# Loading the second expert matrix of the first token tile ahead of the routing table, in a one-core trunk step

## The chip, the cores and the metric

The kernel runs on one core of one Trainium2 chip. The metric is the device time of one execution in microseconds; where a median is given, it is that of three executions. TensorE is called PE, VectorE DVE, ScalarE ACT, GpSimd POOL and SyncE SP. PE multiplies; DVE and ACT do elementwise work; SP issues most of the weight loads; POOL issues the gathers of token rows.

## The reference

One layer of a decoder trunk for 512 prompt tokens and 8 sample tokens, all in float32. A token mixer comes first, then the sub-layer that this change concerns, a mixture of 16 experts in 4 groups, with two experts for each token:

```
gidx = argmax(softmax(hf @ rg + rg_b))            # one group of four
sel  = logits of the four experts of that group
tv, ti = top_k(softmax(sel), 2)                   # two experts inside the group
for e in range(16):
    act = silu(hf @ w1[e]) * (hf @ w3[e])         # w1, w3: 1024 x 512
    y  += (act @ w2[e]) * comb[:, e]              # w2: 512 x 1024
x = x + g2 * y                                    # then a final RMSNorm
```

## The kernel before

**Tiles.** The kernel sorts the 1040 (token, expert) choices into tiles of 128 rows, each for a single expert. In this run there are 18 tiles. Which expert a tile belongs to is known only once the routing table (`table`, `tile_expert`, `fresh_flags`) has been worked out by DVE; the first tile always belongs to expert 0, since no expert is left out of the sort.

**Weights and their ring.** A matrix of an expert (2 MB) comes in four quarters of 512 KB (128 partitions x 1024 floats). A turn of the ring has `TURN = 12` quarters: six places in `raw` and six in `more_raw` (five in `region_a`, one in `region_b`). Before PE can use a quarter, ACT copies it rounded into `w_hi` (`hi`, L1096) and DVE takes the rest into `w_lo` (`lo`, L1519); both have `SPLIT = 4` places. PE then does three products for each pair (`three`, L636 to L638), since operands of the reduced kind are split in two parts.

**Order of the expert stage.** Turn 0 holds w1 and w3 of tile 0 and w1 of tile 1 (ring numbers 0 to 3, 4 to 7, 8 to 11, SP L596, L599, L610). Turn j, from 1 on, holds w3 of tile j, w2 of tile j-1 and w1 of tile j+1 (SP L614 to L617). So the second matrix of tile 0, w2[0], is used in turn 1, at ring numbers 4 to 7. A load whose matrix is the same expert's as the tile's before is left out and only its mark is set by a 4-byte transfer (`kept_mark`, L581). The loops over turns run with register counters, on SP, PE, ACT and DVE alike.

**What stands ahead of the loop.** While the second norm and the routing run, SP loads w1 and w3 of tile 0 and eight quarters of another matrix, the last two column groups of w_ada (`gap_load`, L587), whose products (`gap_products`, L932) fill gaps on PE. The last three of them are issued after `h2_ready` (L600 to L603). Then SP waits for the table (L604), for the first gather and for the gap products (L608, L609), and loads w1 of tile 1.

**Rows of a tile.** The normed token rows h2 are stored to DRAM (L1290, from three buffers in `region_b` that take turns; the traces call the DRAM tensor h_rows). For each tile POOL gathers 128 rows of 4 KB from it into `xg` in `region_b` (L1460, an indirect DMA), PE turns them (L1021 for the first tile, L980 after), ACT and DVE split them into `hT_hi` and `hT_lo`. The first gather needs only the list of expert 0's tokens and starts before the table is complete. The second needs the full list, which DVE and PE work out after the first gather has been turned: split of the first rows (L1978 to L1980), `tile_parts` (L1984), the product in `list_tokens` (L988), `slot_tokens` (L1989), `slot_idx` (L1892). POOL sets `second_begun` (L1467) after it has issued the second gather, and SP starts the loads of turn 1 only then (L613).

SP's, ACT's and POOL's transfers run on the same 16 DMA engines, in three queues: q1 (SP), q10 (ACT), q0 (POOL).

Of the kernel before, what the change touches and what calls it, by code (L numbers as in the profile page):

```python
# [22 lines left out]
P = 128  # L23
# [6 lines left out]
NTILE = NP // P + 1  # L30
# [11 lines left out]
KF = FF // P  # L42
# [8 lines left out]
QUARTER = 1024  # L51
TURN = 12
# [19 lines left out]
N_EXP = N_WO + 8  # L72
# [16 lines left out]
def trunk_step(nc, x_prompt, x_sample, state_conf, state_pool, state_sconv, c_prompt, c_sample, w_ada,  # L89
# [9 lines left out]
    with ctx:  # L99
        def sb(name, shape, dt=F32):  # L100
            return ctx.enter_context(nc.sbuf_tensor(name, shape, dt))

        def sem(name):
            return ctx.enter_context(nc.semaphore(name))
# [3 lines left out]
        w_hi = sb("w_hi", [P, SPLIT, QUARTER], F32R)  # L108
        w_lo = sb("w_lo", [P, SPLIT, QUARTER], F32R)
# [4 lines left out]
        region_b = sb("region_b", [P, 13500])  # L114
# [24 lines left out]
        table = sb("table", [P, 3], I32)  # L139
        kept_mark = sb("kept_mark", [1, TURN], I32)  # L140
        tile_expert = sb("tile_expert", [P, MAX_TILES], I32)

        fresh_flags = sb("fresh_flags", [P, 2, MAX_TILES], I32)
# [6 lines left out]
        def carve(region, at, *dims):  # L150
            n = int(np.prod(dims))
            v = region[:, at:at + n]
            if len(dims) == 2:
                return v.rearrange("p (a b) -> p a b", b=dims[1])
            if len(dims) == 3:
                return v.rearrange("p (a b c) -> p a b c", b=dims[1], c=dims[2])
            return v
# [5 lines left out]
        def raw_place(n, turn=None):  # L163

            if n < N_APART:
                count, step = 1, TURN // RAW
                place, ready = nat_place[n], apart_ready[n]  # L170
            elif n < N_EXP:
                m = n - N_APART
                count, step = m // RAW + 1, TURN // RAW
                place = raw[:, m % RAW, :]
                ready = raw_ready[m % RAW]
            else:
                c, base = n - N_EXP, N_EXP - N_APART
                if c % TURN < RAW:
                    s = (base + c % TURN) % RAW
                    place, ready = raw[:, s, :], raw_ready[s]  # L180
                    count = (base - s + RAW - 1) // RAW + c // TURN + 1
                else:
                    place, ready = more_raw[c % TURN - RAW], more_ready[c % TURN - RAW]
                    count = c // TURN + 1
                step = 1
            return place, ready, 16 * count if turn is None else turn * (16 * step) + 16 * count

        def split_slot(n):

            return (n - (n > N_MIX)) % SPLIT  # L190

        def splits(n):

            return n + 1 - (n > N_MIX)
# [51 lines left out]
        g2_dec = carve(region_b, 11264, D)  # L246
        yg = [carve(region_b, at, 2, D) for at in (9216, 0, 5120, 7168)]
        more_raw.append(carve(region_b, 2048, QUARTER))
        gap_place = [carve(region_b, 7168, QUARTER), carve(region_b, 8192, QUARTER), carve(region_b, 11264, QUARTER), more_raw[4],
                     carve(region_b, 6144, QUARTER), more_raw[2], more_raw[3], more_raw[5]]  # L250
        g2_rows = g2_dec[0:ND + 1, :]
# [41 lines left out]
        lo_done = sem("lo_done")  # L293
# [45 lines left out]
        h2_stored = [sem(f"h2_stored{i}") for i in range(3)]  # L339
        h2T_done = sem("h2T_done")  # L340
# [17 lines left out]
        table_ready = sem("table_ready")  # L358
        xg_ready = sem("xg_ready")
        second_begun = sem("second_begun")  # L360
        gather_free = sem("gather_free")
        xgT_done = sem("xgT_done")
        silu_ready = sem("silu_ready")
# [97 lines left out]
        def _(sp):  # L461
# [64 lines left out]
            for b, w in enumerate((sc_out, conf_pw)):  # L526
                for q in range(4):
                    n = N_MIX + 1 + 4 * b + q
# [4 lines left out]
            for h in range(2):  # L533
                for q in range(4):
                    n = N_WO + 4 * h + q
# [51 lines left out]
            def gap_load(h):  # L587

                g, q = G_ADA - 1 - h // 4, 2 * (h % 4)
                sp.dma_start(gap_place[h].rearrange("p (k n) -> p k n", k=2), ada_v[:, q:q + 2, g * COLS:(g + 1) * COLS]).then_inc(nat_ready[h], 16)  # L590
# [10 lines left out]
            gap_load(5)  # L601
            gap_load(6)
            gap_load(7)  # L603
            sp.wait_ge(table_ready, 6)  # L604
            last = sp.value_load(table[0:1, 1:2], min_val=NE - 1, max_val=MAX_TILES - 1)
            before_last = sp.value_load(table[0:1, 2:3], min_val=NE - 2, max_val=MAX_TILES - 2)
# [4 lines left out]
            sp.dma_start(g2_bias, b_ada[0, 5 * D:6 * D].partition_broadcast(ND + 1)).then_inc(ld_mod, 16)  # L611

            sp.wait_ge(second_begun, 1)  # L613
            with sp.Fori(1, last) as j:  # L614
                where_fresh(up_weights, 0, exp_w3, bass.ds(j, 1), j, 1)
                where_fresh(down_weights, 4, None, bass.ds(j - 1, 1), j, 0)
                where_fresh(up_weights, 8, exp_w1, bass.ds(j + 1, 1), j, 0)  # L617
# [462 lines left out]
        def _(act):  # L1080
# [5 lines left out]
                ins.then_inc(act_step, 1)  # L1086
                act.wait_ge(act_step, steps[0])

            def hi(n, turn=None):


                place, ready, count = raw_place(n, turn)
                act.wait_ge(ready, count)
                if splits(n) > SPLIT or turn is not None:
                    act.wait_ge(quarter_used, splits(n) - SPLIT if turn is None else turn * TURN + (splits(n) - SPLIT))
                act.activation(w_hi[:, split_slot(n), :], place, ACT.Copy).then_inc(hi_done, 1)  # L1096
# [175 lines left out]
            def his(first, end, j=None):  # L1272
                for c in range(first, end):
                    hi(N_EXP + c, j)
# [50 lines left out]
            def silu_tile(j):  # L1325

                act.wait_ge(quarter_used, TURN * j + splits(N_EXP - 1))
                act.wait_ge(act_ready, j)
                act.activation(silu_t, ps[:, 0, :], ACT.Silu).then_inc(silu_ready, 1)

            def turned_rows_out(j):
                act.wait_ge(xgT_done, j + 1)
                act.activation(xgT_hi, ps[:, 2:4, :].rearrange("p b (k t) -> p (b k) t", k=4), ACT.Copy).then_inc(xgT_hi_done, 1)
# [18 lines left out]
            last = act.value_load(table[0:1, 1:2], min_val=NE - 1, max_val=MAX_TILES - 1)  # L1352
# [13 lines left out]
            his(10, 12)  # L1366
            turned_product_out(0)
            his(12, 15)
            with act.Fori(1, last) as j:
                his(3, 4, j)  # L1370
                silu_tile(j)
                his(4, 8, j)
                turned_rows_out(j + 1)
                his(8, 11, j)
                y_out(j - 1, TURN * j + splits(N_EXP + 7))
                turned_product_out(j)
                his(11, 12, j)
                y_store(j, j - 1)
                his(12, 15, j)
            his(3, 4, last)  # L1380
            silu_tile(last)
            his(4, 11, last)
# [22 lines left out]
            for i in range(NTILE + 2):  # L1405
                if i < NTILE:
                    scale_first(i)
                if i >= 2:
                    t = i - 2
                    n = rows(t)  # L1410
# [75 lines left out]
        def _(dve):  # L1486
# [30 lines left out]
            def rest(out, whole, first):  # L1517

                return dve.tensor_tensor(out, whole, first.bitcast(F32), ALU.subtract)  # L1519

            def lo(n, turn=None):

                count = splits(n) if turn is None else turn * TURN + splits(n)

                dve.wait_ge(hi_done, count)
                rest(w_lo[:, split_slot(n), :], raw_place(n)[0], w_hi[:, split_slot(n), :]).then_inc(lo_done, 1)


            dve.memset(cT[:, :, 16:C_LO].bitcast(F32), 0.0)
# [84 lines left out]
            for n in range(5):  # L1614
                lo(n)
# [110 lines left out]
            for n in range(N_HEAD + 6, N_MIX):  # L1726
                kind, g = ITEMS[n // 4]
                q = 4 * g + n % 4 if kind == "z" else -1
# [95 lines left out]
            def los(first, end, j=None):  # L1824
                for c in range(first, end):
                    lo(N_EXP + c, j)
# [42 lines left out]
            for i in range(NTILE + 1):  # L1869
# [6 lines left out]
                    row_means(i, i, NTILE + i + 1, 3 + i)  # L1876
                if i >= 3:
                    logit_tile(i - 3)
            dve.memset(fresh_flags[:, 0, 0:1], 1)
            dve.memset(fresh_flags[:, 1, 0:2], 1)  # L1880
            dve.tensor_copy(tile_f, tile_no[:, 0:MAX_TILES])
            dve.tensor_scalar(tile_start[:, :], tile_no[:, :], float(P), None, ALU.mult)
# [59 lines left out]
            count, tiles = ps[:, 7, NTILE * NE:(NTILE + 1) * NE], tiles16[:, 8:]  # L1942
# [10 lines left out]
            link(dve.tensor_tensor(ended, ends[:, None, :].broadcast_to([P, MAX_TILES, NE]), tile_f[:, :, None].broadcast_to([P, MAX_TILES, NE]), ALU.is_le))  # L1953
            link(dve.tensor_reduce(tile_f, ended, AX.X, ALU.add))
            dve.tensor_copy(tile_expert[:, :], tile_f).then_inc(table_ready, 1)
            for flags, first in ((0, 1), (1, 2)):
                dve.tensor_tensor(fresh_flags[:, flags, first:], tile_f[:, first:], tile_f[:, first - 1:MAX_TILES - 1], ALU.not_equal).then_inc(table_ready, 1)
            dve.tensor_scalar(table[:, 1:2], ends[:, NE - 1:NE], -1.0, None, ALU.add).then_inc(table_ready, 1)
            dve.tensor_scalar(table[:, 2:3], ends[:, NE - 1:NE], -2.0, None, ALU.add).then_inc(table_ready, 1)
# [35 lines left out]
            def product_tile(j, used):  # L1995

                dve.wait_ge(quarter_used, used)
                dve.wait_ge(silu_ready, j + 1)
                dve.wait_ge(actT_done, j)
                dve.tensor_tensor(act_t, ps[:, 1, :], silu_t, ALU.mult).then_inc(act_ready, 1)  # L2000
# [10 lines left out]
            last = dve.value_load(table[0:1, 1:2], min_val=NE - 1, max_val=MAX_TILES - 1)  # L2011
# [14 lines left out]
            link(dve.reciprocal(share[:, 0, :], col1[:, :, 4]))  # L2026
            link(dve.tensor_tensor(share[:, 1, :], share[:, 0, :], col1[:, :, 5], ALU.mult), share_ready, 1)
            los(12, 15)
            with dve.Fori(1, last) as j:
                los(3, 7, j)  # L2030
                product_tile(j, TURN * j + splits(N_EXP + 3))
                los(7, 8, j)
                turned_rows_rest(j + 1)

                list_out(bass.ds(j + 2, 1))
                los(8, 11, j)
                turned_product_rest(j)
                los(11, 15, j)
            los(3, 7, last)
            product_tile(last, TURN * last + splits(N_EXP + 3))  # L2040
            los(7, 11, last)
# [12 lines left out]
            for i in range(NTILE + 2):  # L2054
                if i < NTILE:
                    n = rows(i)
# [42 lines left out]
```

## Time and profile before

| | |
|---|---|
| median of 3 executions | 883.67 us (883.58 to 884.1) |
| the profiled execution: its time | 885.43 us |
| the profiled execution: its span | 883.6 us |
| PE busy | 820.7 us, 93% of the span |
| DVE busy | 681.3 us, 77% |
| ACT busy | 467.0 us, 53% |
| DMA moved | 201.21 MB, mean 228 GB/s |
| mean granted clock of PE | 0.968 |

Starts are counted from the span's start. The expert stage begins near 507 us, with the first gathered rows. PE's share of the chain that ended last is 81%. The DMA share is high in the first slices of the span and from about 500 us to 830 us. A release named in brackets is what ended an idle time.

### The profile page before, as it was taken

The page shows a single profiled execution, that of the slowest core. Times are in us where ns is not written, and L with a number is a line of the kernel's source. Part 1 is how long each engine was busy: PE and PEld are TensorE (multiplying, and loading weights), DVE is VectorE, ACT ScalarE, POOL GpSimd, SP SyncE. Part 2 cuts the span into 40 slices and gives each one's busy share as a digit, 9 for nine tenths or more (in the row PEclk, how much of TensorE's full clock was granted, in tenths as well). Part 3 has the DMA queues.
Part 4 walks back from the last instruction along what each step waited for, and adds up shares of the span by engine and source line. Part 5 has one row for each costly group of instructions (what it writes and reads, how often), then busy time and mean ns, then how long its engine had stood idle before and what let it go on. Part 6 is the DMA issues. An engine that isn't in the chain of part 4 may idle for free.

```text
span 883.6 us, 14769 instructions
## 1 busy us (share of the span) xinstructions
PE 820.7 (93%) x4987; PEld 692.2 (78%) x4987; DVE 681.3 (77%) x933; ACT 467.0 (53%) x551; POOL 50.1 (6%) x58
## 2 busy tenths in 40 slices
PE   7899999999999999999999989999999999999810
PEld 2589999989899999899776367888888888888700
DVE  0782637978797786698358879998999989998748
ACT  4552442343422221642223368888888888888642
POOL 0002000000000000230000010001000100000040
PEclk9889999999999999999999999999999999999955
DMA  9858535445543321223752489978978899999462
GB/s 331 278 166 284 196 119 165 127 159 167 170 127 115 96 73 48 69 82 120 270 188 96 169 324 397 397 269 299 387 305 317 320 399 400 396 397 401 171 217 96
DMA packets 90963, 201.21 MB, mean 228 GB/s; under 512 B 8760, under 2 KB 13368, under 8 KB 90886
## 3 DMA queue, kind: packets, MB, share of 16 engines
q1 hardware_dynamic: 78813, 165.25, 53.0%
q0 software_dynamic: 4960, 17.89, 5.6%
q10 hardware_dynamic: 7147, 17.47, 5.3%
q8 instruction: 29, 0.48, 0.2%
q14 instruction: 14, 0.11, 0.0%
HBM read 182.44 MB, written 18.87 MB: 228 GB/s over the span
## 4 chain that ended last, share of the span: by engine, by line
PE 81%; DVE 8%; DMA 4%; ACT 2%; issue 2%; ACTq 1%; SPq 1%; POOL 0%; POOLq 0%; DVEq 0%
PE ps L785 31%; PE ps L636 13%; PE ps L638 13%; PE ps L637 13%; PE ps L865 3%; PE ps L980 2%; DMA region_a<-in_x_prompt_dram 2%; DMA region_b<-h_rows,slot_idx 2%; PE ps L817 2%; DVE w_lo L1519 1%; PE ps L664 1%; PE ps L665 1%; ACT w_hi L1096 1%; PE ps L1015 1%; DVE region_b L2061 1%
## 5 line engine op out<-in xcount | busy, mean ns | idle before, releaser
L1519 DVE TENSOR_TENSOR w_lo<-raw,w_hi 128x1024 fp32r<-128x1024 f32 x202 | 241.4, 1224 | 100.3 <-ACT w_hi L1096 98.3
L1096 ACT ACTIVATE w_hi<-raw 128x1024 fp32r<-128x1024 f32 x202 | 207.9, 1056 | 197.4 <-PE ps L785 150.6
L636 PE MATMUL ps<-w_hi,hT_hi 128*128 128x512 f32 (+1 forms) x512 | 205.2, 401 | 5.4 <-DVE hT_lo L1519 3.7
L638 PE MATMUL ps<-w_hi,hT_lo 128*128 128x512 f32 (+1 forms) x512 | 202.1, 395 | 0.0
L637 PE MATMUL ps<-w_lo,hT_hi 128*128 128x512 f32 (+1 forms) x512 | 201.6, 394 | 0.0
L785 PE MATMUL ps<-hT_hi,w_hi 128*128 128x260 f32 x768 | 156.4, 285 | 1.7 <-DVE w_lo L1519 0.9
L785 PE MATMUL ps<-hT_hi,w_lo 128*128 128x260 f32 x768 | 155.0, 283 | 0.0
L785 PE MATMUL ps<-hT_lo,w_hi 128*128 128x260 f32 x768 | 155.0, 283 | 0.0
L785 PEld LDWEIGHTS ps<-hT_hi,w_hi 128*128 128x128 f32 x768 | 118.9, 189 | 5.0 <-DVE w_lo L1519 3.9
L785 PEld LDWEIGHTS ps<-hT_lo,w_hi 128*128 128x128 f32 x768 | 119.4, 190 | 0.0
L785 PEld LDWEIGHTS ps<-hT_hi,w_lo 128*128 128x128 f32 x768 | 118.9, 189 | 0.0
L636 PEld LDWEIGHTS ps<-w_hi,hT_hi 128*128 128x128 f32 (+1 forms) x512 | 94.6, 185 | 29.8 <-issue 4.0
L638 PEld LDWEIGHTS ps<-w_hi,hT_lo 128*128 128x128 f32 (+1 forms) x512 | 94.5, 184 | 24.1
L1519 DVE TENSOR_TENSOR w_lo<-region_a,w_hi 128x1024 fp32r<-128x1024 f32 x90 | 108.4, 1219 | 5.2 <-ACT w_hi L1096 4.6
L637 PEld LDWEIGHTS ps<-w_lo,hT_hi 128*128 128x128 f32 (+1 forms) x512 | 94.7, 185 | 22.5
L1096 ACT ACTIVATE w_hi<-region_a 128x1024 fp32r<-128x1024 f32 x90 | 95.5, 1062 | 28.3 <-PE ps L638 28.3
L1666 DVE SCALAR_TENSOR_TENSOR region_b<-region_b,pT 128x512 f32<-128x512 f32 x120 | 81.7, 735 | 0.0
L1519 DVE TENSOR_TENSOR hT_lo<-ps,hT_hi 128x512 fp32r<-128x512 f32 (+1 forms) x37 | 34.4, 933 | 16.2 <-ACT hT_hi L1349 12.9
L1460 POOL DMA_INDIRECT region_b<-h_rows,slot_idx x18 | 20.8, 1154 | 383.2 <-DVE slot_idx L1892 273.6
L1203 ACT ACTIVATE region_a<-ps 128x520 f32<-128x520 f32 x24 | 14.5, 606 | 33.7 <-PE ps L785 33.7
L1439 POOL TENSOR_TENSOR hT_lo<-region_b,hT_hi 128x520 fp32r<-128x520 f32 x8 | 12.0, 1525 | 299.4 <-ACT hT_hi L1211 275.5
L664 PE MATMUL ps<-w_hi,cT 128*48 128x512 f32 x64 | 27.0, 422 | 2.0 <-DVE w_lo L1519 1.7
(307 smaller groups left out, 788.0 us busy)
## 6 DMA issues: line engine op xcount, KB each, us to landing
raw<-in_exp_w_dram SPq DMA_DIRECT2D x96, 512.0 KB
region_a<-in_exp_w_dram SPq DMA_DIRECT2D x80, 512.0 KB
raw<-in_w_in_dram SPq DMA_DIRECT2D x48, 512.0 KB
raw<-in_w_ada_dram SPq DMA_DIRECT2D x30, 512.0 KB
expert_rows<-region_b ACTq DMA_DIRECT2D x18, 512.0 KB, 6.5
region_b<-in_exp_w_dram SPq DMA_DIRECT2D x16, 512.0 KB
region_b<-in_w_ada_dram SPq DMA_DIRECT2D x14, 512.0 KB, 9.2
expert_rows<-region_a POOLq DMA_DIRECT2D x8, 512.0 KB, 8.1
```

Of the source, the lines that this page charges most:

```text
L636: pe.matmul(out, pairs[0], moving[0], start=start, stop=False)
L637: pe.matmul(out, pairs[0], moving[1], start=False, stop=False)
L638: return pe.matmul(out, pairs[1], moving[0], start=False, stop=stop)
L664: pe.matmul(ps[0:C_LO + 16, bank, :], cT[:, kk, :], hi[:, k, :], start=(kk == 0), stop=False)
L785: mm = pe.matmul(ps[:, 2 * m + h, 0:HT], w[:, k, ms], x[:, kk, h * HT:(h + 1) * HT], start=start, stop=stop)
L817: mm = pe.matmul(ps[:, 2 * s + h, 0:HT], lhs(k), rhs(k)[:, h * HT:(h + 1) * HT], start=(k == 0), stop=(k == n - 1))
L865: mm = pe.matmul(ps[:, 2 * s + h, 0:HT], w[:, k, (t % 2) * P:(t % 2 + 1) * P], x[:, kk, h * HT:(h + 1) * HT], start=start, stop=stop)
L980: t = pe.transpose(ps[:, 2 + k // 4, (k % 4) * P:(k % 4 + 1) * P], xg[:, k * P:(k + 1) * P], ident[:, :])
L1096: act.activation(w_hi[:, split_slot(n), :], place, ACT.Copy).then_inc(hi_done, 1)
L1460: pool.indirect_dma_start(xg, None, h2_dram, bass.IndirectOffsetOnAxis(ap=slot_idx[:, :], axis=0)).then_inc(xg_ready, 16)
L1519: return dve.tensor_tensor(out, whole, first.bitcast(F32), ALU.subtract)
L1666: dve.scalar_tensor_tensor(va[:, c, 0:NP], ua[:, c, t:t + NP], w, va[:, c, 0:NP], ALU.mult, ALU.add).then_inc(conv_step, 1)
```

## The change

Four places of 512 KB in `region_b` get a second use, `early_raw`: two that held vectors for the sample tokens (9216, 10240) and two of the three h2 buffers (0, 1024). SP loads w2 of expert 0 into them right after the last gap loads and ahead of its wait for the table. It waits first until the five h2 tiles have been turned by PE and the two buffers' stores to DRAM have landed. Turn 1 is written out of the loops on SP, ACT and DVE; the loops begin at 2. In turn 1 ACT and DVE split the quarters 4 to 7 from the early places. The ring's places keep their count of marks, so SP sets four marks there. The flag of turn 1 for w2 is no longer computed. PE's and POOL's code is not touched.

```
+        early_raw = [carve(region_b, at, QUARTER) for at in (9216, 10240, 0, 1024)]
...
             gap_load(5)
             gap_load(6)
             gap_load(7)
+            sp.wait_ge(h2T_done, NTILE)
+            sp.wait_ge(h2_stored[0], 32)
+            sp.wait_ge(h2_stored[1], 32)
+            for q in range(KF):
+                sp.dma_start(early_raw[q], exp_w2[0, 0, q * P:(q + 1) * P, :]).then_inc(early_ready, 16)
             sp.wait_ge(table_ready, 6)
...
             sp.wait_ge(second_begun, 1)
-            with sp.Fori(1, last) as j:
+            where_fresh(up_weights, 0, exp_w3, slice(1, 2), 1, 1)
+            for q in range(4, 8):
+                _, ready, _ = raw_place(N_EXP + q)
+                sp.dma_start(kept_mark[0:1, q:q + 1], table[0:1, 0:1]).then_inc(ready, 16)
+            where_fresh(up_weights, 8, exp_w1, slice(2, 3), 1, 0)
+            with sp.Fori(2, last) as j:
...
-            def hi(n, turn=None):
+            def hi(n, turn=None, early=None):
-                place, ready, count = raw_place(n, turn)
+                place, ready, count = raw_place(n, turn) if early is None else (early_raw[early], early_ready, 64)
...
-            with act.Fori(1, last) as j:
+            def turn_of(j, early=False):
                 his(3, 4, j)
                 silu_tile(j)
-                his(4, 8, j)
+                if early:
+                    for q in range(KF):
+                        hi(N_EXP + 4 + q, j, q)
+                else:
+                    his(4, 8, j)
...
+            turn_of(1, early=True)
+            with act.Fori(2, last) as j:
+                turn_of(j)
...
-            def lo(n, turn=None):
+            def lo(n, turn=None, early=None):
-                rest(w_lo[:, split_slot(n), :], raw_place(n)[0], w_hi[:, split_slot(n), :]).then_inc(lo_done, 1)
+                place = raw_place(n)[0] if early is None else early_raw[early]
+                rest(w_lo[:, split_slot(n), :], place, w_hi[:, split_slot(n), :]).then_inc(lo_done, 1)
...
-            with dve.Fori(1, last) as j:
-                los(3, 7, j)
-                product_tile(j, TURN * j + splits(N_EXP + 3))
-                los(7, 8, j)
+            def turn_of(j, early=False):
+                los(3, 4, j)
+                for q in range(KF):
+                    lo(N_EXP + 4 + q, j, q if early else None)
+                    if q == 2:
+                        product_tile(j, TURN * j + splits(N_EXP + 3))
```

On SP, from the fourth gap load on to the loads of w1 of tile 1, before (region_b and raw are SBUF, in_w_ada_dram and in_exp_w_dram the weights in DRAM):

```order
L590 DMA region_b<-in_w_ada_dram 128x2x512
L472 DMA region_a<-in_exp_w_dram 128x2x512 x2
L590 DMA region_a<-in_w_ada_dram 128x2x512 x2
L590 DMA region_b<-in_w_ada_dram 128x2x512
L605 TENSOR_LOAD table
L605 ISA x2
```

and after:

```order
L593 DMA region_b<-in_w_ada_dram 128x2x512
L475 DMA region_a<-in_exp_w_dram 128x2x512 x2
L593 DMA region_a<-in_w_ada_dram 128x2x512 x2
L593 DMA region_b<-in_w_ada_dram 128x2x512
L611 DMA region_b<-in_exp_w_dram 128x1024 x4
L613 TENSOR_LOAD table
L613 ISA x2
```

Four loads of a quarter each stand between the last gap load and the reading of the table.

On ACT, from the end of turn 0 into turn 1, before (w_hi is the rounded copy, and L1369 is the loop's head):

```order
L1349 ACTIVATE hT_hi<-ps 128x4x128
L1096 ACTIVATE w_hi<-raw 128x1024 x3
L1369 UNCONDITIONAL_BRANCH
L1369 ISA
L1095 ISA
L1096 ACTIVATE w_hi<-raw 128x1024
L1329 ACTIVATE region_b<-ps 128x512
L1095 REGISTER_ALU
L1096 ACTIVATE w_hi<-raw 128x1024
```

and after:

```order
L1362 ACTIVATE hT_hi<-ps 128x4x128
L1109 ACTIVATE w_hi<-raw 128x1024 x4
L1342 ACTIVATE region_b<-ps 128x512
L1109 ACTIVATE w_hi<-region_b 128x1024 x4
L1346 ACTIVATE hT_hi<-ps 128x8x128
L1109 ACTIVATE w_hi<-region_a 128x1024 x3
```

The four copies of w2[0] stand where they stood and read another place; the loop's head has moved one turn further on.

## Rows read from the trace of the kernel before

**Rows 1.** Windows: busy us by engine, clock, DMA share, GB/s, by stage.
```profile
495.50:501.40 5.90, 5.30 (x34) 1.53 (x32) 4.44 (x24) 0.80 (x3) 0.00 (x0) 1.00 0.94 308
501.40:506.80 5.40, 4.46 (x10) 0.89 (x10) 4.99 (x19) 0.00 (x0) 1.02 (x1) 1.00 0.48 170
...
513.00:521.20 8.20, 6.93 (x30) 5.26 (x28) 6.30 (x7) 6.96 (x7) 1.18 (x1) 1.00 1.01 340
...
527.00:584.00 57.00, 56.20 (x264) 45.66 (x263) 52.74 (x57) 47.38 (x51) 3.48 (x3) 1.00 1.04 398
584.00:830.00 246.00, 246.00 (x1145) 201.06 (x1144) 226.41 (x219) 207.09 (x218) 13.93 (x12) 1.00 0.92 347
```
**Rows 2.** Waits of PE, 495 to 880 us: us in total, times, longest.
```profile
PE ps L636 <- DVE hT_lo L1519: 3.7, 2, 2.7
PE ps L980 <- DMA region_b<-h_rows,slot_idx: 1.3, 1, 1.3
PE ps L932 <- DMA region_a<-in_w_ada_dram: 0.8, 1, 0.8
PE ps L636 <- DVE w_lo L1519: 0.8, 1, 0.8
PE ps L1021 <- DMA region_b<-h_rows,slot_idx: 0.6, 1, 0.6
```
**Rows 3.** Chain of waits, 497 to 533 us: start, us, what.
```profile
501.41 5.41 DMA region_b<-h_rows,slot_idx
...
506.86 0.67 PE ps L1021 x4
...
508.18 1.29 DVE hT_lo L1519 x2
...
513.03 8.15 DMA region_b<-h_rows,slot_idx
```
**Rows 4.** Timeline of SP's queue: start, us of issuing, operation.
```profile
495.05 0.47 SPq L590 DMA_DIRECT2D region_b<-in_w_ada_dram  x1
509.70 1.53 SPq L472 DMA_DIRECT2D region_a<-in_exp_w_dram  x3
...
514.80 5.98 SPq L472 DMA_DIRECT2D raw<-in_exp_w_dram  x6
```
**Rows 5.** DMA issues of the page: stores of h2 rows.
```profile
h_rows<-region_b ACTq DMA_DIRECT2D x4, 512.0 KB, 2.6
```
**Rows 6.** The line of the gathers, all 18: issue to landing.
```profile
DMA to landing us min/median/max: 5.4/7.5/8.2
```
**Rows 7.** DMA issues at 525 to 526, then at 614 to 615 us: us to landing.
```profile
region_b<-h_rows,slot_idx POOLq DMA_INDIRECT x1, 7.7
```
```profile
region_b<-h_rows,slot_idx POOLq DMA_INDIRECT x1, 6.2
```
**Rows 8.** Groups from 500 us on, by form: splits by place.
```profile
L1519 DVE TENSOR_TENSOR w_lo<-raw,w_hi 128x1024 fp32r<-128x1024 f32 x106 | 124.9, 1220 | 4.6 <-ACT w_hi L1096 2.8
...
L1519 DVE TENSOR_TENSOR w_lo<-region_b,w_hi 128x1024 fp32r<-128x1024 f32 x18 | 22.1, 1225 | 4.3 <-ACT w_hi L1096 4.3
```
**Rows 9.** Windows of PE alone: busy us, granted clock, DMA share, GB/s.
```profile
488.00:492.00 4.00, 3.75 (x27) 0.99 0.08 14
492.00:495.40 3.40, 3.23 (x20) 0.51 0.30 108
831.00:835.00 4.00, 1.27 (x9) 1.00 0.32 131
840.00:843.50 3.50, 2.40 (x7) 1.00 0.32 130
```
**Rows 10.** Timeline of PE: gap products.
```profile
487.31 1.89 PE L932 MATMUL ps<-region_b,small 128*16 128x512 f32 x4
...
492.71 3.18 PE L932 MATMUL ps<-region_b,small 128*16 128x512 f32 x4
...
505.25 1.02 PE L932 MATMUL ps<-region_b,small 128*16 128x512 f32 x2
```

More of the change, by code:

```diff
@@ L360, in trunk_step @@
         second_begun = sem("second_begun")
+        early_ready = sem("early_ready")
         gather_free = sem("gather_free")
@@ L1878, in _ @@
                     logit_tile(i - 3)
-            dve.memset(fresh_flags[:, 0, 0:1], 1)
+            dve.memset(fresh_flags[:, 0, 0:2], 1)
             dve.memset(fresh_flags[:, 1, 0:2], 1)
@@ L1955, in _ @@
             dve.tensor_copy(tile_expert[:, :], tile_f).then_inc(table_ready, 1)
-            for flags, first in ((0, 1), (1, 2)):
+            for flags, first in ((0, 2), (1, 2)):
                 dve.tensor_tensor(fresh_flags[:, flags, first:], tile_f[:, first:], tile_f[:, first - 1:MAX_TILES - 1], ALU.not_equal).then_inc(table_ready, 1)
@@ L2038, in _ @@
                 los(11, 15, j)
+            turn_of(1, early=True)
+            with dve.Fori(2, last) as j:
+                turn_of(j)
             los(3, 7, last)
```

## The prediction

> **What bounds the kernel now.** I read the windows by stage first. From 527 us to 584 us PE is busy for 56.20 of 57.00 us and from 584 us to 830 us for all of it, although the DMA engines are just as full there (share 1.04 and 0.92) [rows 1]. Then I read PE's waits from 495 us on. They are 7.4 us in all: 3.7 and 0.8 us for DVE, 1.3 and 0.6 us for gathered rows, 0.8 us for a gap load, and what is left is under half a microsecond. None is for a weight quarter of the experts that came late from DRAM; those for DVE are splits that it finished late, one of them the 2.7 us in the last tile [rows 2]. So from turn 1 on the loads are hidden, w2[0]'s with them. Last I read the chain of waits at the entry. It goes through the first gather (501.41, 5.41 us), the turning and splitting of its rows, the list of the second tile's tokens, and the second gather (513.03, 8.15 us) [rows 3]. At this place a transfer is the path, and its length counts one for one.
>
> **Part 1: the four early loads.** SP issues its last gap load at 495.05 us for 0.47 us [rows 4]. The new waits are met by then: these gap loads wait themselves until the last h2 rows are computed, a store of such rows to DRAM lands 2.6 us after its issue [rows 5], and the five turnings precede the routing. So the four loads are issued at once, at about 0.5 us each: 495.5 to 497.5 us. They bring 4 x 0.524 = 2.1 MB. At the rate of a full queue, 398 GB/s [rows 1], that is 5.3 us of all 16 engines. What do they find? Up to 501.4 us the engines are at 0.94 with the gap and w3 loads. From 501.4 to 506.8 us they move 5.4 x 170 = 0.92 MB, of which 0.52 MB are the gather's, so 0.4 MB, or one microsecond, of loads is left at 501.4 us [rows 1]. The added 5.3 us therefore lie from about 502.4 to 507.7 us, and longer with the gather between them. They cover the whole of the first gather, which today has the engines nearly to itself.
>
> What does that cost the gather? Of the 18 gathers this one is the fastest, 5.4 us; the median is 7.5 and the slowest 8.2 [rows 6]. The nearest row is the gather issued at 525.49 us, in the middle of a full queue in which w2[0] itself is being loaded today: 7.7 us. The one at 614.4 us, which starts on idle engines and is joined by loads later, takes 6.2 us [rows 7]. So the first gather grows by 7.7 - 5.4 = 2.3 us; the bounds are 6.2 - 5.4 = 0.8 us and 8.2 - 5.4 = 2.8 us. I take 2.3, since the competitor is the same matrix and there is no idle head.
>
> In the gather's case the row shows 2.3 us beside a queue of more than 5 us. The Trainium skill (DMA: Bandwidth & Descriptors, Queues, rings and completion order) says that each DMA engine goes round robin between the queues that have work, a packet at a time. By that rule the gather isn't put behind all of the 2.1 MB, but it does share with it; were there one line for all, it would be the full 5.3 us later. The trace agrees with the former.
>
> Does anything absorb it? PE has its gap products until 506.27 us and is turned loose by the gather at 506.86 us [rows 3, 10], so 0.6 us of idle time is there already [rows 2] and the delay adds to it. All that follows in the chain (turn, two splits, `tile_parts`, the token list, `slot_idx`) hangs on the gathered rows, and so does the second gather [rows 3]; SP's next loads (509.70 us) wait for the first gather and the last gap product, which stands behind the turning [rows 4]. Everything moves as one block, PE's 1.3 us wait for the second gather with it. After that PE's few waits are for DVE's splits, which move too, and from 527 us on it is without idle time, so nothing is won back. Cost of part 1: +2.3 us.
>
> **Part 2: what is taken out of turn 1.** SP leaves out 2.1 MB after w3[1] and sets four marks of 4 bytes. Today six issues stand from 514.80 to 520.78 us [rows 4], four for w3[1] and two for w2[0]; w1[2] follows. The second gather, issued at 513.03, lands at 521.18 us. What is ahead of it in q1 is w1[1] (issued 509.70 on) and w3[1], which both stay. w2[0] stands behind 2.1 MB of w3[1], that is 5.3 us of work that begins only when w1[1]'s own 5.3 us (to about 516) are done, so it doesn't move before 521 us. Hence the second gather stays at 8.15 us: 0. The bound on the side of a gain is that of the lightest comparable gather, 8.2 - 6.2 = 2.0 us; on the side of a loss 0. From 521 us on w1[2] and the next turns arrive earlier, and nobody waits for them [rows 2]: 0.
>
> **Part 3: splits and the unrolled turn.** ACT and DVE do the same four copies and four subtractions from another place; DVE needs 1225 ns from region_b and 1220 ns from raw [rows 8], which is nothing. The loop head moves from turn 1 to turn 2. If entering a loop costs ACT or DVE something, it is there before and after, and both run up to four quarters ahead of PE; if that cover were gone, it would show as a wait like the 0.8 us one on `w_lo` [rows 2], so I bound it by ±0.8 us and take 0. SP's reading of the table comes after its four added issues (2 us), which end at 497.5 us, well before the table. It is free.
>
> **Sum.** 885.43 + 2.3 + 0 + 0 = 887.7 us for the profiled execution. That execution is 1.76 us above the median of 883.67, so the forecast for the median is 883.67 + 2.3 = 886.0 us, with 885.5 (gather 7.2) to 886.5 us (8.2) as its own range.
>
> **Rivals.**
> B: the same delay, and PE's clock falls. With the gather at 509.1 us PE sits idle from 506.27 us for 2.9 us, and its neighbours are short transposes. The trace is divided: the granted clock fell to half (1.2 of 2.4 GHz) at 492 us after a stretch of short transposes and small products that was nominally busy for 3.75 of 4 us, and near 843.5 us after 2.40 of 3.5 us; but from 831 to 835 us it stayed full with 1.27 of 4 us busy [rows 9]. Its price is in the rows of the gap products: four took 1.89 us at the full clock and 3.18 us at the half one [rows 10], 1.3 us lost in some 3.4 us. Here the turning, the last gap products and the first expert quarter would be hit, all on the path: +2.3 + 1.1 = +3.4 us with a bound of +2.8 + 1.3 = 4.1, so 887.1 us (up to 887.8). The Trainium skill (TensorE: Matmul & The Clock Gate, What's actually happening) has it that the throttled state is the default and activity releases it; the fall at 492 us is in keeping with that, the full clock at 831 us shows that an idle stretch of this length doesn't always suffice.
>
> D: the first gather is hurt only a little, as the one at 614.4 us, because the early loads are nearly done when its packets come: +0.8 us, 884.5 us. For it speaks that the loads are issued six microseconds ahead of the gather; against it that the queue was still working off older loads until 502 us.
>
> C, the other side: the second gather, the longest of the kernel, is held up today by the queue that w3[1] and w2[0] make together, and with w2[0] gone it falls to 6.2 us, -2.0 us. It decides when this is more than what the first gather loses: with +0.8 us there, -1.2 us, 882.5 us; with +2.3 us it is +0.3 us and no change that can be seen. For it speaks that two of w2[0]'s quarters are issued while the gather is still under way; against it that they stand last in their queue.
>
> That the change doesn't do what it says (early loads issued late, after the table) is excluded by the order of SP's waits unless a store lands very late; then it costs as much or nothing.
>
> **How the numbers follow.** Forecast 0.36, B 0.31, D 0.16, C 0.17 (0.10 with a gain that shows, 0.07 cancelled). A change of up to 0.2%, 1.8 us, can't be told from none by a measurement of this kernel. Slower: the forecast and B, 0.67, plus 0.01 of D: 0.68. Same: 0.15 of D, 0.07 of C: 0.22. Faster: 0.10. The range runs from 884.2 us (just under D, leaving out C's gains) to 888.0 us (above B's bound of 887.8); what is left out is about 0.15 below and a few hundredths above. The range of the likeliest cases, forecast and B together, is 885.5 to 887.8 us.
>
> **What would show it.** The first gather: 7.2 to 8.2 us to landing in place of 5.41, and PE's wait at L1021 (its line after) near 2.9 us. The DMA share from 502 to 508 us near 1.0. The second gather unchanged near 8.1 us and the wait of 1.3 us before the second turning kept. A turn's length unchanged, since PE is without idle time there. For B, a stretch at half clock beginning near 509 us. I am wrong if the first gather stays under 6.5 us, if the second drops by over a microsecond, or if DVE, ACT or PE show a new wait at the entry of the loop in turn 2.

## The result, and the profile after

| | before | changed |
|---|---|---|
| median | 884.82 us (20 executions, 881.4 to 886.15) | 888.72 us (20 executions, 885.46 to 891.85) |
| ratio | | 1.0048, 95% interval 1.0038 to 1.0058 |
| profiled execution: time, span | 885.43, 883.6 us | 887.22, 885.3 us |
| mean granted clock of it | 0.968 | 0.972 |

The changed kernel is slower by 0.48%, some 4.2 us, clear of noise. The forecast was a loss of 2.3 us, 886.0 us, with a range up to 888.0. Direction and place were right, the size was not. The kernel before came out a microsecond higher in these 20 executions than in its first three (883.67), so part of the miss in microseconds is that; the ratio says that the loss itself was also nearly twice the forecast.

The stages in the windows that answer to [rows 1], in the changed kernel (the columns are those of that group):

```profile
495.50:501.40 5.90, 5.75 (x32) 1.71 (x29) 4.67 (x23) 0.39 (x1) 1.02 (x1) 1.00 1.01 382
499.00:506.20 7.20, 3.85 (x9) 0.68 (x7) 5.62 (x19) 0.00 (x0) 1.02 (x1) 1.00 0.91 368
501.40:506.80 5.40, 1.97 (x9) 0.72 (x8) 3.40 (x7) 0.00 (x0) 0.00 (x0) 1.00 0.75 306
513.00:521.20 8.20, 6.51 (x29) 4.97 (x28) 5.72 (x5) 6.44 (x7) 0.62 (x1) 1.00 0.99 344
527.00:584.00 57.00, 56.19 (x264) 45.66 (x263) 52.87 (x57) 47.57 (x51) 3.47 (x3) 1.00 1.02 376
584.00:830.00 246.00, 246.00 (x1145) 201.06 (x1144) 226.46 (x219) 206.94 (x219) 13.89 (x12) 1.00 0.92 346
```

In the window that held the first gather before (501.4 to 506.8 us) the engines move 306 GB/s in place of 170, and PE is busy for 1.97 us in place of 4.46. The gather begins earlier in this execution; over its own length, 499.0 to 506.2 us, they move 368 GB/s. From 527 to 830 us PE is as busy as before, although in the first 57 us of it some 1.3 MB fewer are moved (376 GB/s in place of 398). SP's queue shows the order that was asked for:

```profile
492.31 0.47 SPq L593 DMA_DIRECT2D region_b<-in_w_ada_dram  x1
492.89 2.73 SPq L611 DMA_DIRECT2D region_b<-in_exp_w_dram  x4
```

PE's waits from 495 us on, to be held against [rows 2]:

```profile
PE ps L649 <- DVE hT_lo L1541: 3.7, 2, 2.7
PE ps L1034 <- DMA region_b<-h_rows,slot_idx: 3.4, 1, 3.4
PE ps L993 <- DMA region_b<-h_rows,slot_idx: 1.7, 1, 1.7
PE ps L649 <- DVE w_lo L1541: 0.8, 1, 0.8
```

The wait for the first gather has grown from 0.6 to 3.4 us, that for the second from 1.3 to 1.7; those for DVE are the old ones. And the chain of waits, against [rows 3] (start, us, what):

```profile
499.01 7.22 DMA region_b<-h_rows,slot_idx
506.28 0.67 PE ps L1034 x4
...
512.45 8.55 DMA region_b<-h_rows,slot_idx
521.04 1.11 PE ps L993 x8
```

The first gather takes 7.22 us in place of 5.41. In this execution it happens to be issued 2.4 us earlier than in the profile of before, so positions can't be compared, only lengths. From the issue of the first gather to the second turning it is 521.04 - 499.01 = 22.03 us, before 521.23 - 501.41 = 19.82.

A single profile is one draw, so both kernels were profiled once more, and this settled where the rest is.

### The profile page after: what moved, and what is told of

Same layout as the page of the kernel before. It is cut to its first block, busy times and chain, and to the rows that moved or that the text cites. A ratio compares the mean times of both kernels' runs of the same rounds, so it can differ in the third digit from the quotient of the medians.

```text
span 885.3 us, 14707 instructions
## 1 busy us (share of the span) xinstructions
PE 818.1 (92%) x4987; PEld 691.0 (78%) x4987; DVE 681.6 (77%) x933; ACT 467.1 (53%) x551; POOL 50.4 (6%) x58
## 4 chain that ended last, share of the span: by engine, by line
PE 82%; DVE 9%; DMA 4%; issue 2%; ACT 2%; SPq 1%; POOL 0%; ACTq 0%; POOLq 0%; DVEq 0%
PE ps L798 31%; PE ps L649 13%; PE ps L651 13%; PE ps L650 13%; PE ps L878 3%; DMA region_b<-h_rows,slot_idx 2%; PE ps L993 2%; DMA region_a<-in_x_prompt_dram 2%; PE ps L830 2%; DVE w_lo L1541 1%; PE ps L677 1%; PE ps L678 1%; PE ps L1028 1%; ACT w_hi L1109 1%; DVE region_b L2091 1%
## 5 line engine op out<-in xcount | busy, mean ns | idle before, releaser
L1109 ACT ACTIVATE w_hi<-raw 128x1024 fp32r<-128x1024 f32 x200 | 205.7, 1056 | 197.0 <-PE ps L798 150.8
L1541 DVE TENSOR_TENSOR w_lo<-region_a,w_hi 128x1024 fp32r<-128x1024 f32 x88 | 106.0, 1221 | 5.2 <-ACT w_hi L1109 4.6
L1109 ACT ACTIVATE w_hi<-region_a 128x1024 fp32r<-128x1024 f32 x88 | 93.4, 1062 | 27.6 <-PE ps L651 27.6
L1541 DVE TENSOR_TENSOR w_lo<-region_b,w_hi 128x1024 fp32r<-128x1024 f32 x24 | 29.2, 1223 | 4.3 <-ACT w_hi L1109 4.3
```

## The experiments

Each ratio is to runs of the kernel before on the same chip; n is the number of executions. Most intervals are about ±0.15%, so only differences of over a microsecond or two are told apart by times alone; the lengths in the profiles are sharper.

| run | n | median us | before us | ratio (95%) |
|---|---|---|---|---|
| e1 added only | 8 | 888.56 | 884.74 | 1.0046 (1.0027 to 1.0064) |
| e2 places only | 12 | 885.86 | 884.74 | 1.0006 (0.9992 to 1.002) |
| e3 behind the gather | 12 | 885.92 | 884.74 | 1.002 (1.0004 to 1.0035) |
| e4 PE running | 12 | 887.27 | 884.74 | 1.0038 (1.0024 to 1.0052) |
| e5 delay only | 8 | 887.93 | 884.66 | 1.0039 (1.002 to 1.0058) |
| e6 delay, PE running | 12 | 885.61 | 884.66 | 1.001 (0.9994 to 1.0026) |
| e7 half | 12 | 886.3 | 884.66 | 1.0022 (1.0003 to 1.004) |
| e8 w1 early | 12 | 884.02 | 884.66 | 1.0003 (0.9989 to 1.0017) |
| e9 tail running | 12 | 883.44 | 884.74 | 0.9985 (0.9967 to 1.0002) |
| e10 w1 early and tail | 12 | 882.14 | 884.74 | 0.9973 (0.9956 to 0.999) |

**e1: add the loads, take nothing away.**

```
 (kernel before)
+            for q in range(KF):      # ahead of the wait for the table, unused
+                sp.dma_start(early_raw[q], exp_w2[0, 0, ...]).then_inc(early_ready, 16)
```

> The kernel before with the four early loads added and not used: w2[0] is loaded in turn 1 as well, all splits and loops are those of before. Theory (the early loads slow the first gather, and the relief of turn 1 is worth nothing): as slow as the changed kernel, ratio to before 1.004 to 1.006, first gather 7.2 to 8.2 us. Rival (the unrolled turn, the marks or the other places cost time): ratio near 1.000. Rival (the relief of turn 1 wins something back): slower than the changed kernel, over 1.006.

1.0046 against the changed kernel's 1.0048: the four loads alone lose as much as the whole change, and what turn 1 is spared gives nothing back that could be measured. The first gather is as long as in the changed kernel:

```profile
501.99 7.64 DMA region_b<-h_rows,slot_idx
```

(POOL waits once for the added loads, long after the stretch in question, before it gathers the experts' results.)

**e2: everything but the time of issue.**

```
 (changed kernel)
-            (four loads ahead of the table)
             where_fresh(up_weights, 0, exp_w3, slice(1, 2), 1, 1)
+            (the four loads here)
```

> The changed kernel with its four loads of w2[0] issued where they were before the change, right behind w3[1] in turn 1. All else (places, unrolled turn, marks) as changed. Theory: all the loss is in the time of issue, so the ratio to before is 0.999 to 1.001, first gather 5.4 us. Rival (unrolled turn, marks, places cost): 1.002 to 1.005.

1.0006, an interval that holds 1: the places, the marks and the unrolled turn cost nothing that could be measured. Its first gather landed after 4.3 us:

```profile
DMA to landing us min/median/max: 4.3/4.3/4.3
```

That is a microsecond less than the 5.4 us which the forecast took for the gather's length without company.

**e3: the loads behind the first gather.**

```
 (changed kernel)
             sp.wait_ge(xg_ready, 16)
+            (the four loads here)
             sp.wait_ge(gap_used, 4 * G_GAP)
```

> The changed kernel with its four loads issued as soon as the first gather has landed, ahead of w1 of tile 1. Theory: the first gather is back at 5.4 us and the 2.2 us come back; the second gather meets a fuller queue and may lose up to 0.5 us: ratio to before 1.000 to 1.001. Rival (whatever stands ahead in the queue delays w1 of tile 1 enough to stop PE): 1.002 or more, with a wait for DVE's w_lo of tile 1's w1 on PE.

The first gather is at 4.3 us again; the second takes 8.64 us:

```profile
508.52 8.64 DMA region_b<-h_rows,slot_idx
```

1.002 is less than half the loss of the changed kernel, and a little over what was expected. The interval doesn't part it from e2's 1.0006. The wait for `w_lo` that the rival named is not there: in this profile PE waits 0.8 us for `w_lo`, as before.

**e4: PE kept running while it waits.**

```
 (changed kernel)
+            for _ in range(24):
+                pe.transpose(ps[:, 1, 0:P], ident[:, :], ident[:, :])
             pe.wait_ge(xg_ready, 16)
```

> The changed kernel with 24 transposes of the identity on PE, results unused, between the last gap products that don't need the first gather and the wait for it: 2.5 to 2.9 us of work into an idle time of 3 us. Theory (part of the loss is PE's clock falling after the longer idle time in many executions): 1.0 to 2.0 us faster than the changed kernel, ratio to before 1.0025 to 1.0035, with a higher mean granted clock. Rival (the loss is the gather's delay alone, the clock has no part): the same as the changed kernel, 1.0045 to 1.005, or a little slower by what the transposes run over.

1.0038 is in the direction of the theory, a microsecond less than the changed kernel, but the intervals overlap, and it is above the 1.0025 to 1.0035 that was expected. By itself this decides nothing. Its profile has the long gather (7.42 us) and the full clock behind it.

**e5 and e6: the delay without the transfers.**

```
 (kernel before, POOL)
             pool.wait_ge(slot_idx_ready, 1)
+            for t in range(14):
+                pool.memset(delay_cell[:, 0:1], 0.0).then_inc(delay_chain, 1)
+                pool.wait_ge(delay_chain, t + 1)
             gather(0)
 (e6: also 22 transposes on PE as in e4)
```

> The kernel before with its first gather issued some 2.5 us later: POOL writes one cell 14 times, each waiting for the one before, between the list of tokens and the gather. No transfer is added or moved. Theory (a longer idle time of PE costs itself and, by a fall of PE's clock in a part of the executions, over a microsecond more): slower than before by the delay as the profile shows it plus 0.5 to 1.5 us on the mean, so 3.0 to 4.0 us for 2.5. Rival (a delay costs just itself, and what the changed kernel lost beyond it is contention elsewhere): 2.3 to 2.7 us.

> The same delay of the first gather, with 22 unused transposes of the identity on PE ahead of its wait for the gather. Theory: the delay's own 2.5 us is left, 0.5 to 1.5 us less than in the run with the delay alone, and the granted clock doesn't fall near 509 us. Rival (a delay costs just itself): as slow as the run with the delay alone.

The memsets took 2.13 us, and the gather was issued 3.06 us after the first of them began. Since the gather, issued later, was quick (4.3 us), PE's wait for it was 2.7 us, 2.1 more than in [rows 2]. e5 lost 0.39%, 3.5 us; e6, with the same delay and PE running, 0.10%, 0.9 us. The means over the executions are 887.37 and 885.58 us, 1.8 us apart with a standard error of 0.8. The windows of PE alone (busy us, granted clock, DMA share, GB/s), e5 first:

```profile
506.00:508.00 2.00, 0.18 (x2) 1.00 0.41 160
508.00:510.00 2.00, 2.00 (x10) 0.66 0.00 0
...
510.00:512.00 2.00, 2.00 (x5) 0.50 0.00 0
```

and e6:

```profile
506.00:508.00 2.00, 2.00 (x19) 1.00 0.00 0
508.00:510.00 2.00, 1.99 (x7) 1.00 0.00 0
...
510.00:512.00 2.00, 1.95 (x16) 1.00 0.49 166
```

In e5 PE's clock goes to half (1.2 GHz of 2.4) just as the gathered rows arrive; in e6 it stays full. Less of the loss was left in e6 than was expected: 0.9 us, with an interval from -0.5 to 2.3, where the delay's own length of over 2 us was to stay. This isn't explained. Nor do the two profiles show the 1.8 us: in e6 the rows had landed at 505.95 us and PE, still at its unused transposes, turned them at 506.88 us, and from the issue of the first gather to the turning of the third tile's rows it is 36.1 us against 35.0 in e5, since the second gather happened to take 8.5 us against 7.1. So the profiles show the clock, and the gain in time rests on the means alone.

**e7: half of the loads.**

```
-            for q in range(KF):
+            for q in range(2):
                 sp.dma_start(early_raw[q], exp_w2[0, 0, ...]).then_inc(early_ready, 16)
 (quarters 2 and 3 in turn 1, at the ring's places)
```

> The changed kernel with two of the four quarters of w2[0] loaded early and the other two in turn 1 at the ring's places. Theory (queues share the engines): the added queue is gone about 505 us, in the middle of the gather's transfer, so the gather grows by 1.0 to 1.5 us in place of 2 to 3 and the ratio to before is 1.0015 to 1.003. Rival (any queue ahead costs the whole): 1.004 to 1.005.

1.0022. The gather grows less than with all four, by 0.6 us over e2's 4.3 where 1.0 to 1.5 were expected, and PE waits 1.1 us for it:

```profile
500.64 4.87 DMA region_b<-h_rows,slot_idx
...
511.73 8.57 DMA region_b<-h_rows,slot_idx
```

**e8: another matrix in the early places.**

```
 (kernel before)
             sp.wait_ge(xg_ready, 16)
-            sp.wait_ge(gap_used, 4 * G_GAP)
-            up_weights(8, exp_w1, expert_of(slice(1, 2)), None)
+            (w1 of tile 1 into early_raw)
+            sp.wait_ge(gap_used, 4 * G_GAP)
+            (four marks)
```

> Another use of the four early places: the kernel before with w1 of tile 1 loaded into them as soon as the first gather has landed, 2.9 us earlier than today, when the engines are idle; w2[0] stays in turn 1. Theory (gathers are slowed by what is queued on SP's side): the second gather, issued 6 us later, finds most of it done and takes 6 to 7 us in place of 8.2; PE's wait of 1.3 us before the second turning shrinks to 0, so 0.5 to 1.3 us faster than before, ratio 0.9985 to 0.9995. Rival (the second gather is held by w3[1], which is issued behind it): 8 us, ratio 1.000.

The second gather came down to 5.5 us to landing, the line of its issue reading

```profile
region_b<-h_rows,slot_idx POOLq DMA_INDIRECT x1, 5.5
```

and PE no longer waited for it. In time that is too little to be seen: 1.0003. The time from the first gather's issue to the second turning was 516.95 - 499.42 = 17.53 us, against 18.4 to 19.8 us in three profiles with the old order. But e2, whose loads have the old order too, took 517.31 - 499.69 = 17.62 us with a second gather of 6.8 us. So the shorter gather is shown (5.5 us here and 5.3 in e10, 6.5 to 8.6 in all other profiles), a gain for PE isn't.

**e9: PE kept running in the last tile.**

```
 (kernel before)
             turn_product(last)
+            for _ in range(20):
+                pe.transpose(ps[:, 7, 0:P], ident[:, :], ident[:, :])
             w2_of(8, last, last + 1, last)
```

> The kernel before with 20 unused transposes of the identity on PE in the last tile, in the 2.7 us that it waits for the split of the last product. Theory (after an idle time of nearly three microseconds PE's clock falls in a part of the executions, here at the last down product, 5.5 us of matmuls): 0.3 to 1.3 us faster than before on the mean and no half clock between 831 and 840 us. Rival (the clock has no part): the same as before.

0.9985, with an interval that still holds 1. What it does is shown below beside the second profile of before.

**e10: e8 and e9 together.**

> w1 of tile 1 loaded early behind the first gather, together with the unused transposes in the last tile. Theory: both gains add, 1 to 2 us faster than before, ratio 0.998 to 0.999. Rival: the same as before.

0.9973 (0.9956 to 0.999), 2.3 us faster than before by the ratio: a version that beats both kernels. Which of its two parts did it is open: each by itself has an interval that holds 1.

**The two second profiles.**

> The changed kernel once more, for a second profile of it. Theory: first gather 7.2 to 7.7 us, PE idle before it for about 3 us; a fall of the clock behind it, which the first profile doesn't have, is as likely as not.

> The kernel before once more, for a second profile of it. Theory: first gather 4.3 to 5.4 us, PE idle before it for 0.5 us and no fall of the clock behind it.

The changed kernel again (888.23 us), chain of waits, then windows of PE alone:

```profile
500.11 7.64 DMA region_b<-h_rows,slot_idx
...
507.80 1.94 PE ps L1034 x8
...
514.13 0.17 DVE slot_idx L1915
...
515.08 8.35 DMA region_b<-h_rows,slot_idx
...
523.47 1.11 PE ps L993 x8
```

```profile
506.00:508.00 2.00, 0.20 (x1) 0.97 0.51 205
508.00:510.00 2.00, 2.00 (x9) 0.50 0.01 2
```

Here the clock does fall behind the long wait, and the eight transposes take 1.94 us in place of 1.09. From the landed gather to the second gather's issue it is 515.08 - 507.80 = 7.28 us, in the first profiles of both kernels 6.17 us. Before again (886.24 us) has a first gather of 4.4 us, no fall of the clock behind it, and this chain:

```profile
512.15 7.55 DMA region_b<-h_rows,slot_idx
519.75 1.11 PE ps L980 x8
```

It has a fall of the clock elsewhere. In the last tile PE waits 2.7 us for DVE. The second profile of before, timeline of PE:

```profile
830.27 0.60 PE L1015 MATMUL ps<-ident,region_b 128*128 128x128 f32 x4
833.59 0.79 PE L636 MATMUL ps<-w_hi,hT_hi 128*128 128x512 f32 x1 [2.72 <-DVE hT_lo L1519]
840.86 1.98 PE L1075 MATMUL ps<-region_b,small 9*128 9x512 f32 x4
```

and its clock there:

```profile
833.00:837.00 4.00, 3.41 (x8) 0.57 0.21 87
```

The same place in e9:

```profile
831.39 0.60 PE L1015 MATMUL ps<-ident,region_b 128*128 128x128 f32 x4
831.82 2.35 PE L1071 MATMUL ps<-ident 128*128 128x128 f32 x20
834.72 0.49 PE L636 MATMUL ps<-w_hi,hT_hi 128*128 128x512 f32 x1 [0.55 <-DVE hT_lo L1521]
...
840.49 1.98 PE L1077 MATMUL ps<-region_b,small 9*128 9x512 f32 x4
```

From the turning to the last product it is 10.59 us in the one and 9.10 us in the other. In the first profile of before the clock did not fall there [rows 9] and it was 9.09 us, in e9's it didn't fall either. So one fall costs 1.5 us and comes in some executions only. Of the twelve profiles with this wait and no transposes in it, seven take 10.5 to 10.7 us and five 9.1 us, with and without the early loads. The first profile of the changed kernel is one of the seven (831.14 to 841.79 us), so 1.6 us of what parts it from the first profile of before has nothing to do with the change.

## Why the prediction was right in its direction and wrong in its size

In short: the path and the mechanism were right. The step that failed is the size of part 1, a growth of 2.3 us reckoned from one profile's 5.4 us where 2.8 us were measured, and the sum left out the fall of the clock behind it. The working follows.

The stretch from the issue of the first gather to the turning of the third tile's rows is where the change acts. Three profiles have it with the old queue (before twice, e9) and three with the four loads ahead of the gather (changed twice, e1). In us, means with the single values, worked out from the starts in the timelines:

| part | old queue | loads ahead | difference |
|---|---|---|---|
| issue of gather 1 to its turning | 4.8 (5.45, 4.40, 4.42) | 7.5 (7.27, 7.69, 7.68) | 2.8 |
| turning to issue of gather 2 | 6.3 (6.17, 6.39, 6.37) | 6.9 (6.17, 7.28, 7.25) | 0.6 |
| issue of gather 2 to its turning | 8.0 (8.20, 7.60, 8.32) | 8.5 (8.59, 8.39, 8.52) | 0.5 |
| to the next turning | 16.2 (16.22, 16.22, 16.21) | 16.2 (16.22, 16.23, 16.21) | 0.0 |
| sum | 35.3 | 39.2 | 3.8 |

3.8 us from the profiles against 4.2 us (3.4 to 5.1) from the times: the loss is accounted for within what single profiles can tell. Two more profiles bear on the table. e2, with the loads where they were before the change, has 4.37, 6.41, 6.84 and 16.19 us, 33.8 in all; e4, with the loads ahead and PE kept running, has 7.47, 6.17, 6.74 and 16.14 us, 36.5 in all. They bear out the first row and not the third. Now the steps.

- *What bounds the kernel, and part 3.* Right. PE's path runs through the first gather, nothing waits for the loads of turn 1 or later, and e2 shows that places, marks and unrolled code cost nothing measurable.
- *Part 1, the mechanism.* Right: e1 has the loads alone and the whole loss, e3 and e7 lose less with the loads behind the gather or halved. Of the loaded gather's length the forecast (7.7 us; 7.2 to 7.6 measured) was nearly right as well.
- *Part 1, the size.* This is the step that failed: "So the first gather grows by 7.7 - 5.4 = 2.3 us". The 5.4 us were taken as the gather's length on engines that it has "nearly to itself". They were not quite: in that profile a microsecond of loads was still in the queue, as the paragraph ahead had worked out. With no early loads ahead of it the gather takes 4.2 to 4.4 us in seven profiles (before's second, e2, e3, e5, e6, e8, e9) and 5.3 to 5.4 in two (before's first, e10). At its use on PE the term is 2.8 us. Subtracting from a single profile took one execution's draw for the kernel's value. Why the gather took 5.4 us in that draw isn't shown. The loads that were left are not enough to explain it: some 0.4 MB of them went beside the gather there, and in e7 some 1.1 MB (4.9 us at 338 GB/s, less the gather's 0.52 MB), with a gather of only 4.87 us. And this term is only 0.5 us of the 1.9 us between the forecast and the measured loss; by the table another 0.6 us is the clock behind the first gather (rival B below), 0.5 us the second gather, and 0.4 us is in none of the rows.
- *Part 2, the second gather.* Valued at 0; the three and three profiles have +0.5 us, with values that nearly touch, and e2 (6.84) and e4 (6.74) have no difference. Its length was between 5.3 and 8.6 us over all profiles, so that it grew with the change isn't shown. Rival C, that the relief of turn 1 shortens it, isn't borne out: e1 without relief and the changed kernel with it have 8.5 and 8.5 us and nearly the same ratio.
- *Rival B.* It is not the other way it could go but a part of the same loss. PE's clock fell behind the first gather in two of the three profiles with the loads, at a price of 1.1 us each (7.28 and 7.25 against 6.17 us), just the 1.1 us that the rival named, and in none of those with the old queue. e5 against e6 points to the cause: with a delay and no added transfer the clock falls, and with PE running through the wait it stays, each in one profile, and the means lie 1.8 us apart (standard error 0.8). The forecast picked the case without it, while the median contains both: on the mean 0.6 us by the table. Of 831 to 835 us, where the clock stayed full after 2.7 us of idle time [rows 9], the prediction concluded that "an idle stretch of this length doesn't always suffice". That was correct, and the second profile of before completes it: the same stretch, and there the clock falls.
- *The range* ended at 888.0 because its upper end added bounds to a first median of three executions. 20 executions put before 1.15 us higher; 886.0 as a ratio is 1.0026, and 1.0038 is the low end of what was measured. The upper end as a ratio is 1.0049, just over the measured 1.0048; so it is the 1.15 us of the first median that put the measured 888.72 us beyond 888.0, and the place of that bound is luck either way.

## What to carry to other kernels

A load moved into a queue that looks idle is free only if nothing on the path is about to go through the same engines; here four early loads of 0.5 MB made a 4.3 us gather take 7.5 us, and what they relieved later had been hidden anyway. Take the undisturbed length of a short transfer from several profiles, or from the fastest like it, and treat a longer PE wait as costing more than itself, since the clock can fall behind it. If the queue is to be helped, look for the transfer that PE does wait for: w1 of tile 1 in the same four places (e8) shortened the second gather, 7.6 to 8.3 us in three profiles with the old queue, to 5.5 us, where w2 of tile 0 could help no one; by itself even that gained nothing that the times could show.

## What the hardware showed that was not expected

Executions of one program differ by up to 7 us here (before: 880.8 to 888.0 us). One source is visible: stretches at half clock follow the same PE wait in one execution and not in the next, each at 1.1 to 1.6 us. Behind waits of nearly three microseconds that were filled with unused transposes of 128 columns the clock stayed full in the profiles of e4, e6, e9 and e10. In times e6 was 1.8 us (standard error 0.8) faster than e5, and e10, with such transposes and the earlier load, was the fastest kernel of the study, 882.14 us. Not every fall follows a long wait: between 488 and 495 us the clock fell in thirteen of the fourteen profiles (not in e2's), in before's first behind a stretch in which PE was busy for 3.75 of 4 us [rows 9].
